# Modulation weights in row pieces, and a retention stage whose gate products are spread over other work

## What is computed

```python
def modulation(cond, w, b):                      # cond: c for latent tokens, c_ctx for the prompt
    m = silu(cond) @ w + b                       # w_mod[l]: 1024 x 6144, six vectors of 1024
    return split(m, 6)                           # shift1, scale1, gate1, shift2, scale2, gate2
...
h = rms_norm(x, norm1) * (1 + scale1) + shift1
z = h @ w_in                                     # q, k, v | qr, kr, vr, gr | mu, mv | three gates
att = attention(q, k, v)                         # 8 heads, keys: latent + cache; the prompt on its own
ret = head_group_norm(bidir_retention(qr, kr, vr, states), ret_gn) * silu(gr)
cm  = gelu(mu) * (w_spatial @ rms_norm(gelu(mv), mlp_norm) + b_spatial)
x   = x + gate1 * ((sig(g_att)*(att@w_att_o) + sig(g_ret)*(ret@w_ret_o) + sig(g_mlp)*(cm@w_mlp_o)) @ w_out)
x   = x + gate2 * moe(rms_norm(x, norm2) * (1 + scale2) + shift2)    # 16 experts, top 2
```

## Time and profile before

| | us |
|---|---|
| three runs | 2377.09, 2380.5, 2380.65 (median 2380.5) |
| the profiled execution | 2377.39 |
| its span | 2375.6 |
| TensorE busy / mean granted clock | 2141.1 (90%) / 0.948 |
| VectorE, ScalarE, GpSimd busy | 1230.3, 818.0, 266.3 |
| DMA | 417.13 MB, 176 GB/s over the span |

### The profile page before, as it was taken

How to read it: one execution, slowest core, us unless ns; L and a number is a source line. 1 busy time by engine, 2 the same in 40 slices (tenths; PEclk the granted TensorE clock), 3 DMA queues, 4 the chain that set the end, 5 groups by cost and what they waited for, 6 DMA issues and landing times.

```text
span 2375.6 us, 25634 instructions
## 1 busy us (share of the span) xinstructions
PE 2141.1 (90%) x10487; PEld 1604.0 (68%) x10487; DVE 1230.3 (52%) x1630; ACT 818.0 (34%) x1030; POOL 266.3 (11%) x222
## 2 busy tenths in 40 slices
PE   1899989999999969999849999999999996799992
PEld 0587555488886448888627855647888844688881
DVE  0386455322222448888655844532232234788883
ACT  1123533100000127887532155221000011587881
POOL 2133020100000021000031411001000000110002
PEclk9899989999999959999969999999999996799996
DMA  7226440221134269999551337011121133699984
GB/s 264 107 71 226 149 151 1 74 87 71 36 107 160 99 235 370 415 409 412 212 217 36 109 116 240 10 71 54 62 81 72 40 146 142 226 414 415 411 356 151
DMA packets 113912, 417.13 MB, mean 176 GB/s; under 512 B 7801, under 2 KB 9961, under 8 KB 89089
## 3 DMA queue, kind: packets, MB, share of 16 engines
q1 hardware_dynamic: 89088, 329.27, 36.5%
q0 software_dynamic: 19920, 68.31, 7.6%
q10 hardware_dynamic: 4784, 17.87, 1.8%
HBM read 378.89 MB, written 36.54 MB: 175 GB/s over the span
## 4 chain that ended last, share of the span: by engine, by line
PE 88%; DVE 5%; DMA 3%; ACT 1%; issue 1%; SPq 0%; PEldq 0%; POOL 0%; DVEq 0%; ACTq 0%; POOLq 0%
PE ps L655 76%; PE ps L773 3%; PE ps L785 2%; PE ps L666 2%; PE ps L1039 1%; DMA ring_lo<-in_w_mod_dram 1%; PE ps L1050 1%; DMA work<-y_dram,slots_u 1%; DVE work L1627 1%; PE ps L774 1%; DVE work L1902 1%; DVE work L1904 1%; DVE work L1905 1%; SPq L448 0%; DMA work<-h_dram,slots_u 0%
## 5 line engine op out<-in xcount | busy, mean ns | idle before, releaser
L1859 DVE TENSOR_TENSOR expert_low<-ring_lo,expert_high 128x2048 fp32r<-128x2048 f32 x172 | 386.2, 2285 | 2.9 <-ACT expert_high L1392 2.9
L1392 ACT ACTIVATE expert_high<-ring_lo 128x2048 fp32r<-128x2048 f32 x172 | 326.3, 1914 | 108.0 <-PE ps L655 88.4
L655 PE MATMUL ps<-ring_lo,hT 128*128 128x512 f32 (+1 forms) x800 | 315.8, 552 | 12.5 <-ACT hT L1206 12.3
L655 PEld LDWEIGHTS ps<-ring_lo,hT 128*128 128x128 f32 x800 | 150.3, 191 | 160.3 <-issue 156.6
L655 PE MATMUL ps<-expert_high,x_high 128*128 128x512 f32 x512 | 207.6, 405 | 9.6 <-DVE expert_low L1859 9.6
L655 PE MATMUL ps<-branch,ring_lo 128*128 128x320 f32 x768 | 214.4, 432 | 0.0
L655 PE MATMUL ps<-expert_high,x_low 128*128 128x512 f32 x512 | 202.2, 395 | 0.0
L1341 ACT ACTIVATE work<-ps 128x640 f32<-128x640 f32 x48 | 33.8, 704 | 485.5 <-PE ps L655 485.4
L655 PE MATMUL ps<-expert_low,x_high 128*128 128x512 f32 x512 | 200.9, 392 | 0.0
L655 PE MATMUL ps<-h_hi,w_hi 128*128 128x320 f32 x768 | 186.2, 324 | 2.6 <-issue 2.6
L655 PEld LDWEIGHTS ps<-branch,ring_lo 128*128 128x128 f32 x768 | 143.5, 190 | 53.3
(11 more groups left out here) (272 smaller groups left out, 3283.4 us busy)
## 6 DMA issues: line engine op xcount, KB each, us to landing
ring_lo<-in_w_up_dram SPq DMA_DIRECT2D x64, 1024.0 KB, 7.9
ring_lo<-in_w_gate_dram SPq DMA_DIRECT2D x54, 1024.0 KB, 7.6
ring_lo<-in_w_down_dram SPq DMA_DIRECT2D x54, 1024.0 KB, 8.1
ring_lo<-in_w_in_dram SPq DMA_DIRECT2D x26, 2048.0 KB, 8.3
ring_lo<-in_w_mod_dram SPq DMA_DIRECT2D x24, 2048.0 KB, 13.6
y_dram<-branch ACTq DMA_DIRECT2D x32, 512.0 KB, 8.3
work<-in_w_down_dram SPq DMA_DIRECT2D x10, 1024.0 KB, 7.9
work<-in_w_gate_dram SPq DMA_DIRECT2D x10, 1024.0 KB, 8.4
```

Of the source, the lines that this page charges most:

```text
L655: return pe.matmul(out, lhsT, rhs, start=(k == 0), stop=(k == n - 1))
L1392: A(e_high[n % HIGH], e_raw[n % RAW], ACT.Copy).then_inc(ec_a.sem, 1)
L1859: TT(out=e_low[n % RAW], in0=e_raw[n % RAW], in1=e_high[n % HIGH].bitcast(F32), op=ALU.subtract).then_inc(el_v.sem, 1)
```

## The change

1. A modulation load holds 256 rows of all 2048 columns of its group (runs of 8 KB). `mod_group` waits for one piece, uses it (two k), marks it read (`mod_pc`), and goes to the next.
2. The first group's rows are no longer stored and reloaded: their 128 x 512 area is zeroed ahead (POOL), PE turns it with four transposes beside the eight rows of norm1, and DVE copies the wanted columns to `modc` with a second copy.
3. norm1 and w_spatial have a semaphore of their own (`first_inputs`); the other twelve small inputs are issued once the third modulation piece has landed.
4. The gr products stand elsewhere: tile 0 behind unit 33, tile 1 behind two states, tile 2 behind four, tiles 3 and 4 in rounds 0 and 1. `mv` products 0 to 2 stand in rounds 2 to 4. `sgr` has five buffers; tile 1 uses bank 7.
5. In a round q and k of the next tile are turned between scores and output products; `turn_ret` of the former tile comes last. `mv` 3, `turn_ret(4)`, `mv` 4 follow. DVE takes the next q ahead of the statistics. ACT does three SiLU ahead of the rounds, waiting for the modulation stores and the zeroing of y_dram first.

The big product of the round is now one of mv (slot 1), and the turning of q and k stands where `turn_ret` stood. The diff, cut:

```diff
             if key[0] == "mod":
-                return mod_mm, NGRP * key[1] + key[2] // 4 + 1
+                return mod_pc, MODT * key[1] + key[2] + 1
...
-                    return rows(I["w_mod"][key[1], :, key[2] * 512:(key[2] + 1) * 512]), KD, 512
+                    g, j = divmod(key[2], 4)
+                    return rows(I["w_mod"][key[1], 2 * P * j:2 * P * (j + 1), 2048 * g:2048 * (g + 1)]), 2, 2048
...
-        sgr = w_(16896, 512)
+        sgr = [branch[:, 8 * T + 512 * t:8 * T + 512 * (t + 1)] for t in range(NT)]
...
+        def gr_bank(tt):
+            return 7 if tt == 1 else 5
...
-                for j in range(4):
-                    key = ("mod", l, 4 * g + j)
-                    pe.wait_ge(full[slot_of[key]], full_at(key))
                 for k in range(KD):
+                    key = ("mod", l, 4 * g + k // 2)
+                    if k % 2 == 0:
+                        pe.wait_ge(full[slot_of[key]], full_at(key))
+                    wt = slot[slot_of[key]]
                     for j in range(4):
-                        wt = slot[slot_of["mod", l, 4 * g + j]]
...
+                        c = 2048 * (k % 2) + 512 * j
...
+                    if k % 2 == 1:
+                        i.then_inc(mod_pc, 1)
...
-                w(pe, aux_in, l, aux_in.per)
-                w(pe, modr_in, l, 32)
-                pe.transpose(ps[:, 4, 0:40], mod_rows, ident[0:40, 0:40]).then_inc(au_p.sem, 1)
+                w(pe, au_in, l, 32)
+                pe.transpose(ps[:, 4, 0:KD], norm_rows, ident[0:KD, 0:KD])
+                for c in range(4):
+                    i = pe.transpose(ps[:, 6, c * P:(c + 1) * P], mod_area(l, 0)[1][:, c * P:(c + 1) * P], ident)
+                i.then_inc(au_p.sem, 1)
...
+                def gate_ret(tt):
+                    wt = loaded("gr")
+                    if tt >= 2:
+                        w(pe, gr_a, l, tt)
+                    for k in range(KD):
+                        i = mm(bank(gr_bank(tt)), h3[:, k, tok(tt)], wt[:, k * 512:(k + 1) * 512], k, KD)
+                    i.then_inc(gr_p.sem, 1)
...
+                    if u == NS * HQ + 1:
+                        w(pe, hr_g, l, hr_g.per)
+                        gate_ret(0)
...
+                state_product(0)
+                state_product(1)
+                w(pe, at_a, l, NU // 2)
+                gate_ret(1)
+                state_product(2)
+                state_product(3)
+                gate_ret(2)
+                for n in range(4, 8):
+                    state_product(n)
+                w(pe, kv_v, l, 2 * (NS - 1))
+                w(pe, st_a, l, 2)
+                turn_qkr(0)
+                for tt in range(NT):
+                    if tt < 2:
+                        gate_ret(tt + 3)
+                    else:
+                        if tt == 2:
+                            w(pe, kv_v, l, 8)
+                        if tt == 4:
+                            w(pe, rq_v, l, NT)
+                        mlp_product(0, "mv", tt - 2)
+                    inner_product(tt)
+                    if tt + 1 < NT:
+                        turn_qkr(tt + 1)
+                    ret_out(tt)
+                    if tt >= 1:
+                        turn_ret(tt - 1)
...
-                mlp_product(0, "mv", 0)
+                mlp_product(0, "mv", 3)
                 turn_ret(NT - 1)
-                for tt in range(1, NT):
-                    mlp_product(0, "mv", tt)
+                mlp_product(0, "mv", 4)
...
-                act.wait_ge(mod_st, 64 * (NGRP * l + 1))
...
+                act.wait_ge(y_zero, 32)
+                act.wait_ge(mod_st, 128 * (l + 1))
+                for tt in range(3):
+                    silu_ret(tt)
+                take_rk(0)
+                for tt in range(NT):
+                    if tt < 2:
+                        silu_ret(tt + 3)
+                    if tt + 1 < NT:
+                        take_rk(tt + 1)
...
-                V.tensor_copy(modc, bank(4, 40)).then_inc(mc_v.sem, 1)
+                step.mark(V.tensor_copy(modc[:, 32:40], bank(4, KD)))
+                V.tensor_copy(modc[:, 0:32].rearrange("p (s j c) -> p s j c", s=2, j=4),
+                              bank(6).rearrange("p (c j r) -> p r j c", c=4, j=4)[:, 0:2]).then_inc(mc_v.sem, 1)
...
                     w(V, o_p, l, tt + 1)
+                    if tt + 1 < NT:
+                        take_rq(tt + 1)
...
+                    if tt >= 1:
+                        w(V, rt_p, l, tt)
...
+            G.memset(mod_area(0, 0)[1], 0.0).then_inc(zeroed, 1)
+            G.wait_ge(zeroed, 1)
             load_bias(0, 0)
...
+            first_inputs(0)
+            G.wait_ge(full[slot_of["mod", 0, 2]], full_at(("mod", 0, 2)))
             layer_inputs(0)
-            store_mods(0, 0)
-            G.wait_ge(mod_st, 64)
-            first_mod_rows(0)
```

More of the change, by code:

```diff
@@ L234, in trunk @@
         mod_mm = sem("mod_mm")
+        mod_pc = sem("mod_piece_read")
         mod_ev = sem("mod_ev")
@@ L750, in turn_qk @@
                     pe.transpose(ps[:, 2 + tt % 2, 0:P], src, ident).then_inc(qt_p.sem, 1)
+                w(pe, aux_in, l, aux_in.per)
                 for s, name in enumerate(("qr", "kr")):
@@ L826, in _, with state_product @@
                 w(pe, pv_p, l, NU)
-                for n, (_, tt) in enumerate(STATES):
+                def state_product(n):
+                    tt = STATES[n][1]
                     w(pe, kd_g, l, n + 1)
@@ L834, in _, with turn_qkr @@
                     i.then_inc(kv_p.sem, 1)
[L836 to L849, removed]
+                def turn_qkr(tt):
                     for src, b, sig_p, sig_e in ((0, 2, rq_p, rq_v), (1, 3, rk_p, rk_a)):
@@ L855, in _, with inner_product @@
                         i.then_inc(sig_p.sem, 1)
[L856 to L860, removed]
+                def inner_product(tt):
                     w(pe, rq_v, l, tt + 1)
@@ L867, in _, with ret_out @@
                     i.then_inc(in_p.sem, 1)
+                def ret_out(tt):
+                    w(pe, in_v, l, tt + 1)
                     if tt >= 1:
-                        turn_ret(tt - 1)
-                    w(pe, in_v, l, tt + 1)
+                        w(pe, rn_v, l, tt)
                     for h in range(HR):
@@ L878, in _, with turn_ret @@
                     i.then_inc(o_p.sem, 1)
-                w(pe, kv_v, l, 8)
-                w(pe, rq_v, l, NT)
-                w(pe, rk_a, l, NT)
+                def turn_ret(tt):
+                    w(pe, rn_v, l, tt + 1)
+                    if tt == 0:
+                        w(pe, gr_a, l, 2)
+                    if tt >= 1:
+                        w(pe, rt_ev, l, tt)
+                    for c in range(4):
+                        i = pe.transpose(ps[:, 7, c * P:(c + 1) * P], o_tmp[:, c * P:(c + 1) * P], ident)
+                    i.then_inc(rt_p.sem, 1)
                 def mlp_product(s, name, tt):
@@ L1304, in take_ret, with silu_ret, take_rk @@
                     A(retT[:, :, tok(tt)], heads(bank(7)), ACT.Copy).then_inc(rt_ev.sem, 1)
-                for tt in range(NT):
+                def silu_ret(tt):
+                    w(act, gr_p, l, tt + 1)
+                    A(sgr[tt], bank(gr_bank(tt)), ACT.Silu).then_inc(gr_a.sem, 1)
+                def take_rk(tt):
                     w(act, rk_p, l, tt + 1)
@@ L1632, in _, with take_rq @@
                 w(V, kv_out, l, 32)
-                for tt in range(NT):
+                def take_rq(tt):
                     w(V, rq_p, l, tt + 1)
@@ L1638, in _ @@
                     V.tensor_copy(flat(rqT), bank(2)).then_inc(rq_v.sem, 1)
+                take_rq(0)
+                for tt in range(NT):
                     w(V, in_p, l, tt + 1)
@@ L1951, in layer_inputs @@
                 G.dma_start(dist, I["distances"]).then_inc(aux_in.sem, 16)
-            def first_mod_rows(l):
-                for cond in range(2):
-                    G.dma_start(mod_rows[2 * KD * cond:2 * KD * cond + 2 * KD, :],
-                                mod_dram[l, cond, 0:2, :].rearrange("m (k p) -> (m k) p", p=P)
-                                ).then_inc(modr_in.sem, 16)
+            G.memset(mod_area(0, 0)[1], 0.0).then_inc(zeroed, 1)
+            G.wait_ge(zeroed, 1)
             load_bias(0, 0)
@@ L2051, in _ @@
                 if l + 1 < LAYERS:
+                    G.memset(mod_area(l + 1, 0)[1], 0.0).then_inc(zeroed, 1)
+                    G.wait_ge(zeroed, l + 3)
                     load_bias(l + 1, 0)
```

37 lines of the change are left out of this document (18 added, 19 removed).

## The result

The changed kernel takes 2362.8 us (median of four runs, 2362.1 to 2363.2) beside 2378.8 for the kernel before in the same runs: a ratio of 0.9933, 95% interval 0.9917 to 0.9948. It is faster by 16 us, where 27 were forecast, and lies 1.8 above the upper end of the range. All times here are medians of the fast runs; one execution of the kernel with both single edits took 5671.9 us, which no run here explains, and is left out. The profiled execution lost 15.4 us against the one of the earlier trace rows.

What follows compares the result with a forecast made beforehand. TensorE, with 88% of the chain, was taken as the bound, gains coming only from its idle, low-clock or transfer-waiting time. 2377.4 - 22 (start) - 4 (retention) = 2351.4, +1 towards the median: 2352 us; range 2342 to 2361.

Steps and rivals of the forecast that it cites:

- The last piece at 37: Start: last modulation piece lands at about 37 us, from 42.9 less 7.0 (inputs moved), less 1 (longer runs), plus 2 (sharing).
- From there to the projection, 12 us: Start: 12 us from the last piece's landing to the first projection, at 49, including 1.7 for the piece and 1.6 for bias.
- q is there at 48.7 ... I take 1 us of waiting: Start: layer 0's q weight lands at 48.7 us, hardly ahead of its use, so 1 us of waiting.
- a start of -22: Start term of the sum: 22 us saved, the first projection 23 us earlier less 1 us waiting for q.
- rival 4: Start: q weight lands late behind small inputs and x copy; first projection at 58, start -14, total 2360 us; chance 0.08.
- Units and states, +16.3 and +17.7: Each layer, prompt's units to states: low clock and moved gate products lengthen it by 16.3 us; 17.7 is layer 1's figure.
- Rounds, -19.0: Each layer's retention rounds to the end of mv 4: 74.8 us from the fourth gr product, instead of 93.8.
- "Nothing else moves": Rest of the kernel: no change in time, including the modulation groups in attention and the layer change.
- Rival 1: Units and states: clock stays up between gate products, so retention gains 11 us instead of 4; total 2345 us; chance 0.18.
- Rival 3: Start: last piece lands at 43 as before, first projection at 55, start -17; total 2357 us; chance 0.09.
- rival 5: Slower: gate products of tiles 0 to 2 run at the low clock, +41 us, total 2386 us; chance 0.03.
- Rival 2: Retention brings nothing: DVE's states and the wait for gelu 0 take all; +4 us, total 2356 us; chance 0.12.

Runs made afterwards that it cites:

- both single edits: Changed kernel with the x copy and twelve small inputs held until layer 0's q weight landed, and mv 4 written to PSUM bank 5: 2346.8 us.
- the start alone: Kernel before plus only the change's first three points (row pieces, PE turning, small inputs later), states and retention rounds as before: 2361.9 us.
- retention alone: Kernel before plus only the change's points four and five (gr and mv products moved, new round), start as before: 2381.0 us, ratio 1.0013.
- the inputs ahead: Changed kernel with x copy held for q, retention's fillers placed anew and mv 4 in bank 3 (2340.1 us), here with twelve inputs issued at once: 2339.6 us.

## Why the prediction was wrong, point by point

The sum was -26 against the profiled execution, and -15.4 was measured. The start missed by 4.8, retention by 6.8, the layer change gave back 2.1 (with the execution, not with the change) and the tail took 0.9.

- **The last piece at 37**: right (36.3; 34.3 in the kernel with the start alone). The reason was half wrong: the inputs' 7.0 belong to column pieces, and the 2 us for sharing with the inputs don't show above the scatter.
- **From there to the projection, 12 us**: right in sum, by luck in part. With q out of the way it was 46.77 - 34.20 = 12.6. But the 1.7 for the last piece misread: each 0.85 there holds four weight loads, and eight k have 64 rows, eight for each k. So 0.85 is the price of half a k, and a cold piece of two k takes 3.4. It took 3.18 in that run and 3.59 in the changed kernel. The bias took 1.0 where 1.6 was summed, and small terms made up the rest.
- **"q is there at 48.7 ... I take 1 us of waiting"**: this step failed. Q landed at 52.5, and PE stood still for 4.2 us. The sum counted 2.1 MB of q and 1.4 MB of inputs, and named the copy of x without giving it bytes (2.6 MB); with the copy held back q landed at 48.0. The projection began at 52.6, 2.3 later than a start of -22 puts it. This was rival 4's mechanism at a third of its price, and the prediction's own sign of being wrong, a first projection that waits for q.
- **What follows a wait was not priced.** The first projection took 13.01 instead of the 10.56 of the kernel before, another 2.4. That is the rest of the start's miss.
- **Units and states, +16.3 and +17.7**: 17.8 and 18.9. The units were +6.4 for 5.8, the states 26.3 for 26.1; the turning behind them, not summed at the low clock, +0.8 (layer 0).
- **Rounds, -19.0**: -16.9 and -17.1. The rounds themselves were right: from gate product 3 to mv 3 it was 58.2 and 58.1 for 58.0, and from the last turning's start to mv 4 it was the forecast 3.1 (0.45 of turning, 2.7 of waiting). The 32 rows behind it took 1.9 more than at the full clock: this is the mis-sized term, 3.9 us over both layers.
- **"Nothing else moves"**: the layer change moved by -2.1 between the two profiled executions, which other traces show to come and go.
- **Between profiled run and median**: 0.7 measured (2362.1 and 2362.8), 1 forecast.

Rival 1 (the clock stays up) fell: it was at the low level from 310 to 316 us, over the last unit and the first states, and 3.78 for two states shows it. Rival 3 fell with the last piece at 36.3, rival 5 with gate products of 6.87 to 7.27. Rival 2 (retention brings nothing) is what happened, and somewhat more: it set 0 for the retention's -4, the trace has +2.8, and the runs have about +1 (2362.8 against 2361.9 for the start alone) to +2.5 (retention alone). In the sum: 2352 + 4.8 + 6.8 - 2.1 + 0.9 = 2362.4. That is rival 2 together with a part of rival 4; they had chances of their own and no joint one, and the range ended 2 us short of the two together.

## What to carry to other kernels

A wait left on the chain costs its length and may cost what the clock takes from the rows behind it, here 1.9 to 2.8 us after waits of 3.9 to 5.4 (four traces), 0.2 to 1.9 after one of 2.7 (eight places), and nothing after one of 1.1; so price both, and look first for a free PSUM bank or a filler (14.6 us lay between the same idea with and without its waits). When a load comes to the front, count every byte that shares its time with the next load that the chain needs, a copy with no reader included, and hold that back. Rivals that don't exclude each other belong together in the range.

## What had not been expected of the hardware

**Long runs change who is served, and not only how fast.** With row pieces the load of x took 22.3 us from issue to landing, with column pieces 15.0. The small inputs were issued behind x on GpSimd's queue, and in the run with the inputs ahead they landed 28 to 33 us after their issue, at 34 to 46 us, most of them behind the last piece. In the kernel before they landed 15 to 20 us after it, well ahead of the last piece. This fits that holding them back brought 0.4 us with row pieces and 7 with column pieces. The Trainium skill (DMA: Bandwidth & Descriptors, Queues, rings and completion order) says that each DMA engine goes round between its queues a packet at a time, a packet being some 9 to 17 descriptors. If each run is a descriptor and a packet holds as many of them as before, a queue whose runs grow from 2 to 8 KB moves more bytes at each turn, and the queue beside it waits longer. 22.3 against 15.0 agrees in direction; no run here shows the turns themselves. SyncE's own row shows another side of it. The four issues with column pieces, in the kernel before:

```profile
0.72 26.96 SPq L448 DMA_DIRECT2D ring_lo<-in_w_mod_dram  x4
```

and with row pieces, in the changed kernel:

```profile
0.72 2.36 SPq L449 DMA_DIRECT2D ring_lo<-in_w_mod_dram  x4
```

The same 8.4 MB, in runs of 2 KB, held SyncE's sequencer for 27 us; in runs of 8 KB it was done in 2.4. A piece that isn't issued can't ask for its share, so this may be as much of the reason why x came sooner with column pieces; the two were not measured apart.

**Rate.** From 4 to 18 us 419 GB/s were moved with row pieces, and 409 in the earlier trace rows with column pieces, so the runs' length hardly matters for the rate there.
